# Inverting the recurrence's triangular matrices on two 64x64 diagonal blocks instead of one 128x128 matrix

## Time and profile before

| | before |
|---|---|
| time, median of 3 runs | 2474.18 us (2473.22 to 2479.66) |
| time of the profiled execution | 2490.54 us |
| its span | 2488.8 us |
| mean granted TensorE clock | 0.932 |
| PE busy | 2150.5 us (86%) |
| the four waves, from the first L2043 to the last | 1374.44 to about 1567.28 us of the span |

### The profile page before, as it was taken

How to read it: one execution, slowest core, us unless ns; L and a number is a source line. 1 busy time by engine, 2 the same in 40 slices (tenths; PEclk the granted TensorE clock), 3 DMA queues, 4 the chain that set the end, 5 groups by cost and what they waited for, 6 DMA issues and landing times.

```text
span 2488.8 us, 32251 instructions
## 1 busy us (share of the span) xinstructions
PE 2150.5 (86%) x12692; PEld 1731.8 (70%) x12692; DVE 1298.7 (52%) x2259; ACT 778.2 (31%) x1266; POOL 707.5 (28%) x702
## 2 busy tenths in 40 slices
PE   7999989998999999999898999987867667667587
PEld 7998878998998878998776899874523223222235
DVE  5455726446445834453336655456456556566423
ACT  4344434335444434442233222211211122122122
POOL 0000010000001000000005444027577777777750
PEclk9999999999999969999998999998989888889898
DMA  8553316554554306553322000459899999999980
GB/s 292 189 193 124 118 52 203 187 168 157 192 192 124 114 1 194 193 171 115 108 68 85 1 1 1 128 195 378 299 356 376 351 364 373 356 364 368 372 334 17
DMA packets 253778, 489.91 MB, mean 197 GB/s; under 512 B 13872, under 2 KB 173136, under 8 KB 253536
## 3 DMA queue, kind: packets, MB, share of 16 engines
q0 software_dynamic: 73888, 268.53, 28.8%
q1 hardware_dynamic: 176016, 214.32, 26.6%
q10 hardware_dynamic: 3760, 5.51, 0.7%
HBM read 487.23 MB, written 1.05 MB: 196 GB/s over the span
## 4 chain that ended last, share of the span: by engine, by line
PE 65%; POOL 13%; DVE 7%; issue 7%; DMA 4%; ACT 3%; another core or an unknown queue 0%; DVEq 0%; POOLq 0%; ACTq 0%
PE bank L697 64%; POOL arena_sb L2301 10%; POOL con_sb L2301 3%; DMA arena_sb<-peer_v,arena_sb 2%; DMA arena_sb<-peer_u,arena_sb 1%; DVE parts_sb L1714 1%; DMA con_sb<-peer_v,arena_sb 1%; DVE arena_sb L1850 1%; DVE sq_sb L1734 1%; DVE arena_sb L2043 1%; DVE rstd_sb L1729 1%; PE bank L844 1%; DVE xl_sb L1738 1%; ACT parts_sb L1363 1%; DVE parts_sb L1719 0%
## 5 line engine op out<-in xcount | busy, mean ns | idle before, releaser
L697 PE MATMUL bank<-arena_sb 128*128 128x128 f32 (+8 forms) x2680 | 592.7, 399 | 182.4 <-ACT arena_sb L1663 95.6
L697 PEld LDWEIGHTS bank<-arena_sb 128*128 128x128 f32 (+3 forms) x2680 | 376.7, 206 | 393.1 <-issue 270.4
L697 PE MATMUL bank<-xh_sb,parts_sb 128*128 128x256 f32 x3328 | 610.7, 286 | 22.4 <-DVE xl_sb L1738 16.6
L697 PEld LDWEIGHTS bank<-xh_sb,parts_sb 128*128 128x128 f32 x3328 | 517.4, 191 | 31.1 <-issue 23.8
L697 PE MATMUL bank<-xl_sb,parts_sb 128*128 128x256 f32 x1664 | 471.0, 283 | 0.0
L2190 DVE CUSTOM_DVE_ANT_0 sq_sb<-arena_sb 128x1024 f32<-128x1024 f32 x256 | 309.4, 1224 | 269.8 <-DMA arena_sb<-peer_u,arena_sb 243.9
L1714 DVE TENSOR_TENSOR parts_sb<-ring_sb,parts_sb 128x2048 fp32r<-128x2048 f32 x132 | 298.6, 2290 | 192.5 <-ACT parts_sb L1363 192.5
L2301 POOL DMA_INDIRECT arena_sb<-peer_u,arena_sb x256 | 275.5, 1076 | 186.4 <-DVE arena_sb L2160 102.6
L697 PEld LDWEIGHTS bank<-xl_sb,parts_sb 128*128 128x128 f32 x1664 | 318.2, 191 | 0.0
L697 PE MATMUL bank<-xn_sb,ring_sb 128*128 128x256 f32 (+1 forms) x1200 | 274.7, 392 | 10.8 <-DVE xn_sb L1734 8.9
L1363 ACT ACTIVATE parts_sb<-ring_sb 128x2048 fp32r<-128x2048 f32 x132 | 247.9, 1911 | 93.8 <-PE bank L697 92.4
(11 more groups left out here) (245 smaller groups left out, 1955.8 us busy)
## 6 DMA issues: line engine op xcount, KB each, us to landing
ring_sb<-ffn_w_gate SPq DMA_DIRECT2D x44, 1024.0 KB, 5.4
ring_sb<-ffn_w_up SPq DMA_DIRECT2D x44, 1024.0 KB, 6.5
ring_sb<-ffn_w_down SPq DMA_DIRECT2D x44, 1024.0 KB, 5.0
ring_sb<-w_in SPq DMA_DIRECT2D x17, 1024.0 KB, 5.3
ring_sb<-w_in_ab SPq DMA_DIRECT2D x12, 1024.0 KB, 5.3
ring_sb<-w_out SPq DMA_DIRECT2D x12, 1024.0 KB, 4.9
ring_sb<-w_in_cd SPq DMA_DIRECT2D x12, 1024.0 KB, 5.8
ring_sb<-peer_w_q SPq DMA_DIRECT2D x8, 1024.0 KB, 5.3
```

The source lines that it names most:

```text
L697: return pe.matmul(dst, lhsT, rhs, start=start, stop=stop_, skip_group_check=loose)
```

## The change

The 128 tokens of a chunk are taken as two halves of 64. `early` is the half whose inverse the other one needs (`HALF[d]`), `late` the other.

- Levels 0 to 5 work on the two diagonal 64x64 blocks of each head. Each block has its own 64 partitions, so every product of a level becomes two 64x64x64 products, one in array rows and columns 0 to 63 and one in 64 to 127, into the same bank at different partitions. `TNTT`, `WW`, `LV` and the masks are 64 wide instead of 128. A compact copy of the diagonal blocks, `NC[u]`, is made by ACT (two instructions per unit); POOL multiplies it by the level's mask. `LV` has two buffers, and POOL waits for the W of two levels back.
- Level 0's transposes become products with the identity. POOL makes level 0's `LV` straight from `M4` in two instructions per unit, one for each half.
- Level 6 forms the off-diagonal block alone: one 64x64 product for W and one for TT per head, all with K and M of 64, copied to `TO[u]` by DVE. At level 5 DVE writes the late diagonal block to `TO[u]` and the early one to `TNTT[u]`, in two instructions.
- U is two products per head: a 64x64 one for the early half, and one with K = 128, M = 64 for the late half.
- X (the right sides) moves from behind level 6 to between level 0 and level 1, on PE and on ACT.
- The constant table is 960 columns shorter, and the three row buffers of the last stage that lie in it begin at another constant.

```diff
-                    for l in range(7):
+                    early, late = HALF[d], HALF[1 - d]
+                    for l in range(7):
                         for u in range(4):
                             b = fill_begin(pe, ("W", w, l, u))
...
                             for e in range(2):
-                                if l:
-                                    ins = mm(b[:, e * P : (e + 1) * P], LV[u][:, e, :], TNTT[u][:, 0, e, :], True, True)
-                                else:
-                                    ins = pe.transpose(b[:, e * P : (e + 1) * P], LV[u][:, e, :], ident)
+                                cols = HALF[e]
+                                if l == 6:
+                                    ins = mm(b[late, cols], M4[u][early, e, 0, late], TNTT[u][early, 0, e, :], True, True)
+                                    continue
+                                for ps in HALF:
+                                    if l:
+                                        ins = mm(b[ps, cols], LV[u][l % 2][ps, e, :], TNTT[u][ps, 0, e, :], True, True)
+                                    else:
+                                        ins = mm(b[ps, cols], LV[u][0][ps, e, :], ident[ps, ps], True, True)
                             fill_end(ins, ("W", w, l, u))
-                        if l:
+                        if l == 0:
                             for u in range(4):
-                                b = fill_begin(pe, ("TT", w, l, u))
-                                emptied(pe, ("W", w, l, u))
+                                j = 4 * d + u
+                                b = fill_begin(pe, ("X", w, u))
...
+                        for u in range(4):
+                            b = fill_begin(pe, ("TT", w, l, u))
+                            emptied(pe, ("W", w, l, u))
+                            for e in range(2):
+                                if l == 6:
+                                    ins = mm(b[early, HALF[e]], WW[u][late, e, :], TO[u][late, e, :], True, True)
+                                    continue
+                                for ps in HALF:
+                                    mm(b[ps, HALF[e]], TNTT[u][ps, 1, e, :], WW[u][ps, e, :], True, True)
+                                for ps in HALF:
+                                    ins = mm(b[ps, P + e * HD : P + (e + 1) * HD], WW[u][ps, e, :], TNTT[u][ps, 1, e, :], True, True)
+                            fill_end(ins, ("TT", w, l, u))
...
                         for e in range(2):
-                            ins = mm(b[:, e * HD : (e + 1) * HD], TNTT[u][:, 1, e, :], XX[u][:, e * HD : (e + 1) * HD], True, True)
+                            cols = HALF[e]
+                            mm(b[early, cols], TNTT[u][early, 1, e, :], XX[u][early, cols], True, True)
+                            ins = mm(b[late, cols], TO[u][:, e, :], XX[u][:, cols], True, True)
                         fill_end(ins, ("U", w, u))
```

More of the change, by code:

```diff
@@ L58 @@
     ("dilated", 384), ("cos", 256), ("sin", 256), ("turn", 128), ("turn_mla", 32), ("seen", 512),
-    ("level", 2 * 7 * 128), ("inv", 1), ("count", 16), ("one", 1),
+    ("level", 2 * 6 * 64), ("eye", 64), ("inv", 1), ("count", 16), ("one", 1),
 ):
@@ L108, in constants @@
     put("seen", np.concatenate([row < col, row <= col, row > col, row >= col], 1))
-    level = np.zeros((P, 2, 7, P))
-    for l in range(7):
+    level = np.zeros((P, 2, 6, HD))
+    row64, col64 = row % HD, np.arange(HD)[None, :]
+    for l in range(6):
         n = 1 << l
-        same = (row // (2 * n)) == (col // (2 * n))
-        level[:, 0, l] = same & (row // n < col // n)
-        level[:, 1, l] = same & (row // n > col // n)
+        same = (row64 // (2 * n)) == (col64 // (2 * n))
+        level[:, 0, l] = same & (row64 // n < col64 // n)
+        level[:, 1, l] = same & (row64 // n > col64 // n)
     put("level", level.reshape(P, -1))
+    put("eye", row64 == col64)
     inv2 = (np.float32(10000.0) ** (-np.arange(0, 32, 2, dtype=np.float32) / np.float32(32))).astype(np.float32)
@@ L1607, in recurrence @@
                 act.activation(GATES, GATES, ACT.Sigmoid).then_inc(S("gates_ready"), 1)
[L1608 to L1612, removed]
+                for w, (d, c) in enumerate(WAVES):
+                    for u in range(4):
+                        emptied(act, ("gram", w, u, 0))
+                        emptied(act, ("gram", w, u, 1))
+                        for ps in HALF:
+                            act.activation(NC[u][ps, :, :], M4[u][ps, :, 0, ps], ACT.Copy).then_inc(S("blocks_ready"), 1)
                     for u in range(4):
@@ L1615, in recurrence @@
                         give(act.activation(XX[u], b[:, 0:P], ACT.Copy), ("X", w, u))
+                    for l in range(1, 7):
+                        ps = HALF[1 - d] if l == 6 else slice(0, P)
+                        for u in range(4):
+                            b = take(act, ("W", w, l, u))
+                            give(act.activation(WW[u][ps, :, :].rearrange("p a b -> p (a b)"), b[ps, 0:P], ACT.Copy), ("W", w, l, u))
                     for u in range(4):
@@ L2282, in _ @@
             for w, (d, c) in enumerate(WAVES):
-                for l in range(7):
+                for l in range(6):
+                    mask = C("level", HD, (6 * d + l) * HD).unsqueeze(1).broadcast_to([P, 2, HD])
+                    if l == 0:
+                        pool.wait_ge(S("bonus_in_ready"), 4)
+                        if w:
+                            pool.wait_ge(S("level_ready"), 28 * w)
+                    if l == 1:
+                        pool.wait_ge(S("level_ready"), 28 * w + 8)
                     for u in range(4):
```

78 lines of the change are left out of this document (47 added, 31 removed).

## The result

The changed kernel took 2458.17 us (median of 11 runs, 2446.31 to 2468.82) against 2479.13 us for the kernel before on the same chips (11 runs): ratio 0.9924, 95% interval 0.9902 to 0.9946, some 19 us or 0.8%. The forecast was 39 us.

A forecast was written before the change was run, and what follows sets the result against it. PE's rate was taken to bound the five full levels. Per wave 11.3 + 1.8 - 0.2 - 2.7 - 0.35 = 9.85 us, 39.4 in four, so the median goes from 2474.18 to 2435; range 2420 to 2475.

The forecast's parts named there:

- The rate of small products: Levels 1 to 5: 0.030 us a record, taken from ST; a level 3.0 us against 5.36, gain 11.3 a wave.
- rival 1: Levels: opposite quadrants sharing a bank don't overlap, 0.056 us a record; 6 us slower, 2480; chance 0.09.
- Rival 4: Levels: opposite quadrants pair only partly, 0.036 to 0.050 us a record; 2445 to 2472; chance 0.12.
- Rival 2: Levels: the feed of PE bounds, 0.059 us a record, a level 5.7; 14 us slower, 2489; chance 0.09.
- U: U's 16 products each follow a change of tile shape: 4.5 us against 1.8, loss 2.7 a wave.
- The clock: Waves: the clock dips once a wave for 3 to 7 us as before, a time, not a number of instructions.
- Rival 3: Level 0 to the end of O: clock stays at its lower level, about 13 us lost a wave, 2525; chance 0.04.
- The price of a dip: Kernel before, behind the Gram masking: the lower clock costs about 3.4 us of work in a wave.
- X early: X in the slow-clock stretch: two changes of shape, 0.35 us a wave lost; what it slows there it does not slow elsewhere.
- Level 5's split: Level 5: two DVE instructions per unit (0.28 + 0.42, some overlap), 0.5 us more a wave.

The follow-up runs named there:

- e8: Changed kernel with each unit's level products issued all of one quadrant, then all of the other: level 3.52 us, waves 179.6 us, ratio to before 0.9956.
- e1: Changed kernel with U's products grouped by tile shape, two changes of shape instead of sixteen: waves 150.8 us, ratio to before 0.9872.
- e10: Kernel before plus two unread 128x128x256 products in front of each unit's level 0: waves 188.3 us against 192.8, ratio 0.9987.
- e3: Changed kernel with X put back behind level 6 on PE and ACT: waves 164.2 us, ratio to before 0.9932.
- e5: Changed kernel with X moved to between level 5's TT and level 6's W: waves 152.0 us, ratio to before 0.9846.
- e7: Changed kernel with U zero-padded to K = 128, X between levels 5 and 6, and unread filler before level 0: waves 130.9 us, ratio to before 0.9744.
- e4: Changed kernel plus two unread 64x64 products of 384 columns in front of each unit's level 0: waves 157.5 us, ratio to before 0.9888.
- e9: Changed kernel with X between levels 5 and 6 and unread filler before level 0, U as in the change: waves 151.3 us, ratio to before 0.9818.

## Why the prediction was wrong

The time, 2458, lies inside the stated range of 2420 to 2475, but by luck: the upper part of the range stood there for partial pairing, and pairing was full. The loss came from elsewhere.

**The rate of small products: right.** 0.030 us a record was taken from ST, and the levels have it. With it fell rival 1: here products of opposite row halves, written to different partitions of one bank, overlap. Rival 4 (partial pairing) fell with it; e8 alone comes near it, at 0.037. The rule quoted from the Trainium skill (TensorEngine Tiling (Array Packing), Restrictions and Gotchas) does not hold for this case of opposite quadrants; the Grams alone could not have told.

**Rival 2 fell too.** 96 records every 2.92 us for four levels running, with a wait in front of each group of eight or sixteen, is a steady feed of 0.030 a record, not 0.059. The 62 ns of the Trainium skill (TensorE: Matmul & The Clock Gate, Back-to-back issue gap) is twice the spacing of records; a product here has two records, 0.061 us, so what that figure counts stays open.

**U: the size right, what hangs on it missed.** Forecast 4.5 us; measured 4 x 1.03 = 4.1 at full clock, and 4 x 1.61 = 6.4 at the lower one. The loss from changes of shape was in the sum.

**The clock: the step that failed.** The prediction said that the slow stretch "is a time, not a number of instructions" and that the clock would dip "once a wave for 3 to 7 us as before". Rival 3 had the clock low throughout and got 0.04; nobody asked what U and level 6, made sparser by the same edit, would do to a clock that was already seen to fall where PE had 6 and 4 records in 2 us. The term for the second dip was zero. Measured, the second dips are 44 us at the lower clock inside the four waves, worth up to 22; 19 us are missing in the waves (39.4 forecast, 20.5 measured), so the dips can account for the whole, but 19 is a remainder, and no run takes them away alone. e1 gives back 21.6 us by order alone, the changes of shape included. A half-way state between forecast and rival 3 should have been a rival. The rows before could not have settled it: U's products, forecast 0.28 us apart, are some 14 records in 2 us, more than the 6 and 4 in front of the first dip and fewer than the 18 of the 128x128x128 products at clock 1.00. The price of a dip was off as well: e10 gives little more than 1 us a wave for the first one in the kernel before, where 3.4 was read.

**X early: undersized.** It was priced at a loss of 0.35 us a wave. In the waves X in the slow stretch and not before U costs 8.2 us over four against its old place (e3; the whole runs do not show it), 2 a wave, and 20.3 against a place where it covers waits (e5). The reason given was that the stretch is a time and X there slows nothing elsewhere. But with X away the stretch was 3.4 us in place of 6.8 or more in every wave of e3, and the second dip was missing in two.

**Level 5's split: undersized.** DVE's pair paces level 6's W at 0.75 us a unit, and PE is idle for 0.34 us in between. Four units' W then take 3 x 0.75 + 0.22 = 2.5 us, where 0.9 and 0.5 for the split were in the sum: about 1 us a wave, and no effect on the clock was foreseen.

## What to carry to other kernels

Count records per microsecond, not busy share, to see whether PE is sparse, and hold the count against the same shape where it is dense: 12 in 2 us stand against 71 of 64x64 products, while 18 of 128x128x128 ones are full speed. When a change makes one part dense and cheap, look at what stands right behind it: waits of DVE's pace and a run of products that each change the tile shape brought the clock down for 7 to 17 us a wave, and with that went about half of the gain. Put products of one tile shape together, pad with zeros if it takes that, and lay independent products over the waits.

## What the runs showed of the hardware that was not expected

- Opposite 64x64 quadrants ran at 0.030 us a record into the same bank at different partitions; issued in turn they take 2.92 us a level, quadrant by quadrant 3.52.
- A run in which each product changes the tile shape has them 0.26 us apart at 2.4 GHz and 0.40 at 1.2 GHz (1.03 and 1.61 us for four).
- Unread filler products held the clock at 1.00 through all four waves in two kernels (e7 and the kernel before, e10); with U in the changed form (e4, e9) they removed the first dip alone. The Trainium skill (TensorE: Matmul & The Clock Gate, A second HAM failure mode: psum-queue depth-cycling) tells of small idle times between groups of products that bring the clock down. The changed kernel has such idle times in front of its second dip (0.34 us between units of level 6's W), which agrees; in e9 the clock fell with PE shown busy for 2.00 of 2.00 us, which that section does not tell of.
- POOL's mask multiply of 128x256 took 0.91 us while DVE made the forms of T beside it (L2052, L2054), and 0.73 just behind them (e10).
- In the changed kernel and in most of its variants (9 of 12 traces) PE stops inside the levels in one wave of the four, in e1 in two, for 0.5 to 1 us, with nothing shown that it waits for. From wave 1's timeline of the changed kernel:

```profile
1444.15 2.73 PE L704 MATMUL bank<-arena_sb 64*64 64x64 f32 x88 [0.97 <-issue]
```

What this is stays open; no run was made for it.
